# Mixture-of-experts stage: one fixed 128-row tile for each expert, weights loaded from the routing stage on, in place of a loop over a computed list of tiles

## The reference, cut to what matters

```python
def _moe(h, w_router, b_router, w_gu, w_down):
    t = h.reshape(B * L, D)                                  # D = 1024
    probs = jax.nn.softmax((t @ w_router).astype(F32), axis=-1)   # 16 experts, 4 groups of 4
    sel = probs + b_router
    grp_score = lax.top_k(sel.reshape(-1, 4, 4), 2)[0].sum(-1)
    gsel = jnp.argmax(grp_score, axis=-1)
    in_grp = (jnp.arange(16) // 4)[None, :] == gsel[:, None]
    _, eidx = lax.top_k(jnp.where(in_grp, sel, -jnp.inf), 2)      # two experts of one group
    w = jnp.take_along_axis(probs, eidx, axis=-1)
    w = w / w.sum(-1, keepdims=True)
    gates = jnp.sum(jax.nn.one_hot(eidx, 16) * w[..., None], axis=1)
    gu = jnp.einsum('td,edf->tef', t, w_gu)                  # w_gu: 16 x 1024 x 512
    act = jax.nn.silu(gu[..., :256]) * gu[..., 256:]
    act = act * gates[..., None]
    y = jnp.einsum('tef,efd->td', act, w_down)               # w_down: 16 x 256 x 1024
```

## Time and profile before

| | us |
|---|---|
| median of 3 runs (lowest, highest) | 2418.91 (2414.42, 2424.68) |
| the profiled execution, its own time | 2408.83 |
| its span, first to last instruction | 2407.0 |
| TensorE busy | 1984.3 (82% of the span) |
| VectorE, ScalarE, GpSimd busy | 811.7, 385.5, 356.7 |
| DMA, mean over the span | 159 GB/s |

### The profile page before, as it was taken

The page is one execution under the profiler, slowest core; times in us unless marked ns, Lnnn a source line. Parts: engine busy times, 40 slices in busy tenths (PEclk is TensorE's granted clock), DMA queues, the critical chain, the costliest instruction groups (busy, mean ns, idle before and its releaser), DMA issues. The chain is left out here.

```text
span 2407.0 us, 33215 instructions
## 1 busy us (share of the span) xinstructions
PE 1984.3 (82%) x13493; PEld 1098.1 (46%) x13493; DVE 811.7 (34%) x1666; ACT 385.5 (16%) x872; POOL 356.7 (15%) x476
## 2 busy tenths in 40 slices
PE   5999999998896799737988898898986769759980
PEld 3443434333343444326655655655754634334430
DVE  0123233233423200053255535535535414320007
ACT  1000100000000111132132232232221100011110
POOL 0010101101022000122030031031021002300004
PEclk9999999999998799956998998998895889869995
DMA  9625344350602699793222113023034480159974
GB/s 334 226 83 204 125 146 167 114 175 34 253 40 81 223 350 348 277 347 104 70 85 77 58 52 112 19 85 97 30 113 142 153 255 35 40 183 343 343 258 166
DMA packets 221242, 381.86 MB, mean 159 GB/s; under 512 B 17165, under 2 KB 88469, under 8 KB 221078
## 3 DMA queue, kind: packets, MB, share of 16 engines
q1 hardware_dynamic: 214002, 354.22, 42.3%
q0 software_dynamic: 7104, 25.69, 2.8%
HBM read 305.25 MB, written 74.63 MB: 158 GB/s over the span
## 5 line engine op out<-in xcount | busy, mean ns | idle before, releaser
L545 PE MATMUL bank<-ring,hT 128*128 128x512 f32 x768 | 345.1, 600 | 3.1 <-PEq L262 2.0
L1272 PE MATMUL bank<-hT,ring 128*128 128x272 f32 x1024 | 309.8, 438 | 1.3 <-PEq L879 1.3
L2213 PE MATMUL bank<-ring,exp_xT 128*128 128x512 f32 x512 | 232.8, 608 | 18.3 <-issue 14.6
L545 PEld LDWEIGHTS bank<-ring,hT 128*128 128x128 f32 x768 | 142.3, 191 | 188.3 <-issue 185.6
L1272 PEld LDWEIGHTS bank<-hT,ring 128*128 128x128 f32 x1024 | 196.4, 207 | 56.0 <-issue 21.2
L2791 PE MATMUL bank<-ring,oT 128*128 128x512 f32 x384 | 175.3, 618 | 13.2 <-DMA oT<-oT_spill 12.6
L2213 PEld LDWEIGHTS bank<-ring,exp_xT 128*128 128x128 f32 x512 | 96.8, 194 | 134.9 <-issue 129.9
L2791 PEld LDWEIGHTS bank<-ring,oT 128*128 128x128 f32 x384 | 75.7, 199 | 108.2 <-issue 95.2
L2232 PE MATMUL bank<-ring,exp_aT 128*128 128x512 f32 x256 | 115.4, 593 | 1.6 <-ACT exp_aT L2267 1.6
L1269 PE MATMUL bank<-ring,hT 128*128 128x512 f32 x256 | 112.9, 602 | 0.0
L2302 DVE TENSOR_TENSOR exp_a<-bank,exp_sg 128x256 f32<-128x256 f32 x32 | 13.6, 425 | 278.1 <-ACT exp_sg L2285 278.1
(11 more groups left out here) (437 smaller groups left out, 2535.1 us busy)
## 6 DMA issues: line engine op xcount, KB each, us to landing
ring<-in_moe_w_gu_dram SPq DMA_DIRECT2D x32, 2048.0 KB, 9.3
ring<-in_w_ada_dram SPq DMA_DIRECT2D x24, 2048.0 KB, 9.5
ring<-in_moe_w_down_dram SPq DMA_DIRECT2D x32, 1024.0 KB, 11.6
ring<-in_ret_w_in_dram SPq DMA_DIRECT2D x8, 2048.0 KB, 13.5
ret_Ss<-in_state_ret_dram SPq DMA_DIRECT2D x32, 512.0 KB, 5.1
out_dram<-ret_Ss SPq DMA_DIRECT2D x32, 512.0 KB, 3.9
expert_outputs<-exp_y SPq DMA_DIRECT2D x32, 512.0 KB, 4.7
ring<-in_dn_w_in_dram SPq DMA_DIRECT2D x8, 2048.0 KB, 9.1
```

Source lines behind the costliest of these rows:

```text
L545: last = pe.matmul(ps[u % 2][:, :], core.hT[:, k, tok(t)], core.ring[:, w % RING, k, :], start=(k == 0), stop=(k == KD - 1))
L1272: mm = pe.matmul(ps[U % 2][:, 0:HALF], core.ring[:, w % RING, k, c * P:(c + 1) * P], core.hT[:, k, half * HALF:(half + 1) * HALF], start=( ...
L2213: last = pe.matmul(ps[v][:, :], xT[:, v, k, :], wgu[v][:, k, :], start=(k == 0), stop=(k == KD - 1))
```

## The change

Slots become fixed: each of the 16 experts owns 128 slots, so tile e is expert e; pairs beyond 128 of an expert go to further tiles, which a loop after the 16 handles (none with these inputs, by the counts above). The 16 tiles are written out on every engine, with no registers. There are four buffers for weights in memory of their own (three new, one in the free end of `oT`), so the ring stays free. SP issues the loads of experts 0 to 3 in the routing stage without waiting for the plan, and from then on the loads for expert e+4 as soon as expert e's are used. In layer 0 it also loads `w_ada` block 13 in the routing stage, before it writes modulation 11, and blocks 14 and 15 in the experts stage; their products move to the front of the combine stage. VectorE's list for the rest's tiles is shorter and moves behind the one-hot tables.

```diff
+G = 128
+SHARE = 1
+CAP = G * SHARE
+WAVES = NE * CAP // P
+MAXO = 2 * NTOK // (CAP + 1)
+MAXT = WAVES + MAXO
+SLOTS = 4
...
@@ routing, sync
                     core.load(sp, core.ada_w[12])
                     core.biases_in(sp, 11, 1, res[:, 0:1])
                     core.biases_in(sp, 12, 4, res[:, 1:5])
-                    sp.wait_ge(core.ada_done, 13)
-                sp.wait_ge(planned, 1)
-                for v in range(2):
-                    e = plan.expert(sp, v)
-                    plan.up_weights(sp, e, v)
-                    if v == 0:
-                        plan.down_weights(sp, e, v)
+                for e in range(SLOTS):
+                    plan.fetch(sp, 0, e)
+                    plan.fetch(sp, 1, e)
                 if l == 0:
+                    core.load(sp, core.ada_w[13])
                     core.modulations_out(sp, 11, 1, res[:, 0:1])
@@ routing, vector
-                chain(dve.tensor_copy(dest[:], ps[0][:, 0:NT * NE].rearrange("p (t e) -> p t e", t=NT)))
+                ranks = ps[0][:, 0:NT * NE].rearrange("p (t e) -> p t e", t=NT)
+                chain.mark(dve.tensor_tensor(dest[:], ranks, row(main, NT), ALU.add))
...
-                chain(dve.tensor_tensor(end[:], start[:], nt[:], ALU.add))
-                chain(dve.tensor_scalar(start[:], start[:], float(P), None, ALU.mult))
-                chain(dve.tensor_tensor(dest[:], dest[:], row(start[:], NT), ALU.add))
+                chain.mark(dve.tensor_tensor(end[:], start[:], nt[:], ALU.add))
+                chain(dve.scalar_tensor_tensor(start[:], start[:], float(P), rest, ALU.mult, ALU.add))
+                chain(dve.scalar_tensor_tensor(t16[:], ranks, float(CAP), row(start[:], NT), ALU.is_ge, ALU.mult))
+                chain(dve.tensor_tensor(dest[:], dest[:], t16[:], ALU.add))
...
-                chain(dve.tensor_tensor(exp_t[:], row(end[:], MAXT), bc(tiles, NE), ALU.is_le))
-                chain(dve.tensor_reduce(exp_f[:, 0:MAXT], exp_t[:], AX.X, ALU.add))
-                chain(dve.tensor_scalar(exp_f[:, 0:MAXT], exp_f[:, 0:MAXT], float(NE - 1), None, ALU.min))
-                (and three more, ending in the copy to plan.experts)
...          # after the one-hot tables and keep_modulation:
+                chain.mark(dve.tensor_copy(exp_f[:, MAXO:MAXO + 1], end[:, NE - 1:NE]))
+                chain(dve.tensor_tensor(exp_t[:], row(end[:], MAXO), bc(tiles, NE), ALU.is_le))
+                chain(dve.tensor_reduce(exp_f[:, 0:MAXO], exp_t[:], AX.X, ALU.add))
+                chain(dve.tensor_scalar(exp_f[:, 0:MAXO], exp_f[:, 0:MAXO], float(NE - 1), None, ALU.min))
+                dve.tensor_copy(plan.experts[:], exp_f[0:1, :]).then_inc(planned, 1)
@@ experts, sync
+                for i in range(WAVES + 2):
+                    if i >= 2:
+                        for e in range(NE):
+                            if last_wave(e) == i - 2:
+                                plan.fetch(sp, 1, e + SLOTS, s["y_done"])
+                        sp.wait_ge(s["y_kept_act"], i - 1)
+                        sp.wait_ge(s["y_kept_dve"], i - 1)
+                        sp.dma_start(yr[:, i - 2, :], y[:, i % 2, :]).then_inc(s[f"y_out{i % 2}"], 16)
+                    for e in range(NE):
+                        if last_wave(e) == i:
+                            plan.fetch(sp, 0, e + SLOTS, s["gu_done"])
+                    if l == 0 and i in (7, 9):
+                        core.load(sp, core.ada_w[14 + (i == 9)])
+                for v in range(2):
+                    sp.wait_ge(s[f"y_out{v}"], 16 * (WAVES // 2))
+                sp.sem_inc(s["more_y_out"], 16)
+                with more(sp) as p:            # Fori(0, value_load(number of further tiles))
...
@@ experts, tensor
+                for i in range(WAVES):
+                    turn(i)
+                    if i >= 2:
+                        down(i - 2)
+                    if i:
+                        turn_a(i - 1)
+                    up(i)
+                down(WAVES - 2)
+                turn_a(WAVES - 1)
+                down(WAVES - 1)
+                with more(pe) as p:
...
@@ experts, gpsimd
+                for i in range(2, WAVES):
+                    pool.wait_ge(s["turned"], i - 1)
+                    plan.gather(pool, i, i % 2)
@@ combine_features, tensor
+                for n in range(13, 16):
+                    core.modulate(pe, n, ps[n - 9])
                 for t in range(NT):
-                    if t == 3:
-                        core.modulate(pe, 13, ps[4])
                     pe.wait_ge(s["scaled"], t + 1)
                     if t >= 2:
                         pe.wait_ge(s["kept"], 2 * (t - 1))
                     turn_tile(pe, core, x[:, t, :], t, (2 * (t % 2), 2 * (t % 2) + 1)).then_inc(s["turned"], 1)
-                for n in (14, 15):
-                    core.modulate(pe, n, ps[n - 9])
@@ Plan
+    def fetch(self, sp, half, last, done=None):
+        while self.fetched[half] <= min(last, NE - 1):
+            e = self.fetched[half]
+            if e >= SLOTS:
+                sp.wait_ge(done, last_wave(e - SLOTS) + 1)
+            to, src = ((self.wgu, self.gu), (self.wdn, self.dn))[half]
+            sp.dma_start(to[e % SLOTS], src[:, e]).then_inc((self.gu_in, self.dn_in)[half][e % SLOTS], 16)
+            self.fetched[half] += 1
```

More of the change, by code:

```diff
@@ L2155, in experts, with more @@
         y = st.sb("y", [P, 2, D])
-        names = ("turned", "xT_kept", "gu_done", "silu_done",
-                 "a_done", "aT_turned", "aT_kept", "y_done", "y_kept_act", "y_kept_dve", "y_out0", "y_out1", "stores")
+        names = ("turned", "xT_kept", "gu_done", "silu_done", "a_done", "aT_turned", "aT_kept", "y_done", "y_kept_act",
+                 "y_kept_dve", "y_out0", "y_out1", "more_gu_in", "more_dn_in", "more_turned", "more_xT_kept",
+                 "more_gu_done", "more_silu_done", "more_a_done", "more_aT_turned", "more_aT_kept", "more_y_done",
+                 "more_y_kept_act", "more_y_kept_dve", "more_y_out", "stores")
         s = {n: st.sem(n) for n in names}
+        s["more_x_in"] = st.pool_sem("more_x_in")
         yr = d["y_rows"].rearrange("(s p) n -> p s n", p=P)
[L2161 to L2166, removed]
-                for v in range(2):
-                    step(p * 2 + v, v, p, False)
-            return last
+        def more(eng):
+            return eng.Fori(0, eng.value_load(plan.experts[0:1, MAXO:MAXO + 1], min_val=0, max_val=MAXO))
         with nc.Block() as block:
@@ L2189, in _ @@
-                last = tiles(sp, step)
-                sp.wait_ge(s["y_done"], last * 2 + 1)
-                plan.down_weights(sp, plan.expert(sp, last * 2 + 1), 1)
-                for v in range(2):
-                    keep_rows(last * 2 + v, v)
-                for v in range(2):
-                    sp.wait_ge(s[f"y_out{v}"], last * 16 + 32)
-                    sp.sem_inc(s["stores"], 1)
-            def turn(pe, i, v, p, early):
-                pe.wait_ge(plan.x_in[v], p * 16 + 16)
-                if not (early and v == 0):
-                    pe.wait_ge(s["xT_kept"], i * 2)
-                for k in range(KD):
-                    last = pe.transpose(ps[4 + k // 4][:, (k % 4) * P:(k % 4 + 1) * P], x[:, v, k * P:(k + 1) * P],
-                                        core.ident[:, :])
-                last.then_inc(s["turned"], 1)
@@ L2248, in _, with turn @@
-                turn_a(pe, last * 2 + 1, 1, False)
-                down(pe, last * 2 + 1, 1, last + 1, False)
+                def turn(i):
+                    v = i % 2
+                    pe.wait_ge(plan.x_in[v], 16 * (i // 2 + 1))
+                    if i:
+                        pe.wait_ge(s["xT_kept"], 2 * i)
+                    for k in range(KD):
+                        last = pe.transpose(ps[4 + k // 4][:, (k % 4) * P:(k % 4 + 1) * P], x[:, v, k * P:(k + 1) * P],
+                                            core.ident[:, :])
+                    last.then_inc(s["turned"], 1)
@@ L2311, in _ @@
                 st.clear_used(pool)
-                for v in range(2):
-                    pool.sem_inc(s[f"y_out{v}"], 16)
-                last = pool.value_load(plan.experts[0:1, MAXT:MAXT + 1], min_val=1, max_val=MAXT // 2 - 1)
-                with pool.Fori(1, last + 1) as p:
-                    for v in range(2):
-                        pool.wait_ge(s["turned"], p * 2 + (v - 1))
-                        plan.gather(pool, p * 2 + v, v)
+                for i in range(2, WAVES):
+                    pool.wait_ge(s["turned"], i - 1)
+                    plan.gather(pool, i, i % 2)
+                pool.wait_ge(s["turned"], WAVES)
+                pool.sem_inc(s["more_turned"], 1)
+                with more(pool) as p:
+                    pool.wait_ge(s["more_turned"], p + 1)
+                    plan.gather(pool, p + WAVES, 0, s["more_x_in"])
 def combine(core, l, plan, x_from, x_to):
@@ L2981, in moe_half @@
     mixer_end(core, l, core.oT, x_from, x_mid, plan, logits)
```

(7 more changed lines are left out.)

254 lines of the change are left out of this document (147 added, 107 removed).

## The result

The changed kernel takes 2455.48 us (median of 4 runs, 2453.50 to 2458.67) against 2417.89 (median of 4, 2414.42 to 2424.68) for the kernel before: a ratio of 1.0153, 95% interval 1.0128 to 1.0179. It is 1.5% slower. 2407 was forecast, with 2391 to 2424 as the range.

A forecast was written before the change was run, and what follows sets the result against it. The prediction took TensorE, busy for 82% of the span, to bound the kernel, with transfers a close second. Layer 0 +0.7 and layer 1 -12.7 us gave -12.0: 2396.8 profiled, 2407 as median, range 2391 to 2424.

The forecast's parts named there:

- the exit of the experts stage: End of each experts stage: SP loads the count of further tiles and passes an empty loop, +1.0 us a layer.
- B: Rival, experts stages: stores land late behind the weights and hold up the down product; +24 us, 2431; chance 0.08.
- The pace of the tiles: Experts stages: weights issued earlier bring every tile to 11.40 us, -8.4 us in layer 0 and -11.4 in layer 1.
- SP held in the routing of layer 0: Layer 0 routing: SP waits in the issue behind queued weights, so the experts stage's transposes begin 9.5 us later.
- Rival A: Layer 0 routing: SP is not held, the tiles begin 2.3 us early; -11.8 us more, 2395; chance 0.15.
- VectorE's list and the gathers: Routing: VectorE's shorter list gives -2.0 us in layer 1, gathers behind queued weights cost +0.5.
- The combine stage of layer 0: Products moved from the end of the stage to its front save 1.4 us.
- C: Rival, routing: gathers wait for the whole queue, +7 us in layer 0 and +2 in layer 1; 2416; chance 0.07.

The follow-up runs named there:

- count0: The changed kernel with the count of further tiles written as the constant 0 in place of the computed one: 2446.20 us (one run).
- count2: The changed kernel with the count of further tiles written as the constant 2: 2515.57 us (one run).
- guard: The changed kernel with the loop over further tiles inside a branch taken only for a count above 0, on each engine: 2401.15 us, ratio 0.9954.
- slots2: The changed kernel without the loop over further tiles and with two weight buffers in place of four, in SP's new order: 2383.82 us (one run).
- late_fetch: no_more with layer 0's weights of experts 2 and 3 and `w_ada` block 13 issued at the start of the experts stage: 2380.87 us, ratio 0.9870.
- best_both: guard with late_fetch's order, the count loaded early on SP and GpSimd, and only two experts fetched in layer 1's routing too: 2372.89 us, ratio 0.9846.
- no_more: The changed kernel without the loop over further tiles, on every engine: 2394.75 us, ratio 0.9942.
- comb_back: late_fetch with the products of blocks 13 to 15 in layer 0's combine stage where the kernel before has them: 2378.67 us (one run).
- late_ada: no_more with only `w_ada` block 13 moved to the start of layer 0's experts stage: 2384.12 us (one run).

## Why the prediction was wrong, and where it was right

**The step that failed** is the exit of the experts stage: SP would "load the count of further tiles and pass an empty loop", at 1.0 us a layer, because "the counts (at most 84 pairs for an expert) leave the loop empty". The counts are right and the conclusion is not: the loop's body runs once before its bound ends it, as count0 and count2 show, and a count of 0 costs a pass of 30.4 to 32.4 us. The step should have been sized as a whole tile with nothing beside it, +62.8 us in both layers together instead of +2.0. Nor would 1.0 us a layer have held for a loop that is passed: in guard, where the branch skips it, the load of the count and the branches cost 3.5 and 2.4 us, beyond the bound of 2. The kernel before was evidence to read: its loop ran from 1 to the count + 1 with a smallest count of 1, and so never met this case. None of the rivals had it; B, the one on the side of slower, put the loss elsewhere. The rows that were read could not show it, since before has no such pass, but they price it: a landing of 8.6 us for up weights, an up and a down product, two sets of transposes and a store.

**The pace of the tiles** was right in size: forecast -8.4 and -11.4, measured -9.64 and -11.60 (with the first two tiles), at 11.40 us a turn. Of the cause, slots2 shows that it lies in SP's list and not in the number of buffers or the transfers' rate (331 to 341 GB/s in the changed kernel). The prediction read the stretch from 837.67 to 840.00 as order alone; the two register loads in it, which the change drops as well, stand beside the order as a cause that no run tells apart.

**SP held in the routing of layer 0**, the term that the prediction said decides: forecast +9.5 net, measured +9.96; the last small DMA was put at 819.3 us, 45.65 after the start of routing (819.3 - 773.65), and is through 45.73 after it (824.24 - 778.51). late_fetch confirms the cause. That the two times agree to 0.1 us is in part luck: counted as in the prediction, 15.8 MB were issued ahead of the last down weights and 13.0 MB of them moved when SP came free at 815.57, so 2.9 MB were left and not 3.2, and the engines moved 413 GB/s up to there and not 394; the two errors nearly cancel. Rival A is refuted with it: the Trainium skill (DMA: Bandwidth & Descriptors, "Issuing engines are not separate DMA queues") calls the time to initiate a DMA usually small beside the transfer. With some 2 MB queued this trace agrees, 0.39 us for 2048 KB at 785.64; with several MB queued it does not, 8.93 us for 1024 KB at 798.87.

**VectorE's list and the gathers**: forecast -2.3 for the entry of layer 1 with the register load, measured -3.46. In layer 1 `source` is written 22.67 us after the start of routing instead of 24.59, -1.92 against the forecast -2.0. The gathers' +0.5 was worth more (best_both wins 2.2 with 6.3 MB less ahead of them), and the rest of the entry gave back more than that; by what was not taken apart.

**The combine stage of layer 0**: forecast -1.4. In no_more the stretch behind the tiles is 1.39 us shorter than before, and comb_back gives 1.42 back. The exit in no_more costs nothing against the kernel before, as layer 1 shows (68.31 against 68.26 us behind the tiles), so this is the products alone.

**Rivals B and C**: row stores do land later, 10.3 us in the median (4.7 before), but two tiles are 22.8 us and no down product waits. The gathers did not wait for the whole queue: the entry of layer 1 is 32.5 us and not the 35.6 that C gives (2137.5 - 2101.9).

Summed up by the terms that hold, the forecast without the loop would have been -14.0 us; no_more came out at 2394.75 - 2410.45 = -15.7, and its trace is 14.8 us shorter than that of the kernel before.

## What to carry to other kernels

Before a data-dependent loop is priced at nothing for a count of 0, find out where it tests its bound, and count the stores or gathers in the profile afterwards: one number in the list of transfers shows an unwanted pass. Here a bound of 0 gave one pass of 30 to 32 us. An early prefetch is paid for by whatever small DMA the same engine has to issue behind it; issue first what others wait for, then the megabytes. More buffers, another order of issue and fewer register loads arrived in one change here: try each by itself, the order with the old number of buffers first.

## What the runs showed of the hardware that was not expected

The price of SP's issue grows with what is queued and is paid by the DMA behind a large piece, be it large or small: of the four small DMAs of modulation 11 the first takes 6.27 us behind 2048 KB in the changed kernel, all four take 2.31 us behind 1024 KB in late_ada. 12.6 MB of weights that start to go out at 785.64 keep SP until 815.57, 29.9 us, where late_fetch's up weights of the third expert go out at 810.21 on a short queue in 0.40 us. A branch around code that is not run was not free either: with the count loaded early on SP and GpSimd, 2.4 us were left in layer 0 and 0.6 in layer 1, and why the two differ is open. After 14 us of almost no work TensorE's clock was granted at its lower level (0.50) for about 4 us of the loop's up product, which took 9.30 us in layer 0 and 9.62 in layer 1 where a steady one takes 7.03.
